# Splitting the squared activations inside the first MLP product instead of before the second

## What is computed

```python
h = x * (1 + sc2) + sh2
m = jnp.square(jax.nn.relu(h @ pl['w_mlp1'])) @ pl['w_mlp2']   # 1024 -> 4096 -> 1024
x = _layer_norm(DEEPNORM_ALPHA * x + g2 * m, pl['ln2_g'], pl['ln2_b'])
```

## Time and profile before

| quantity | value |
|---|---|
| median of 3 runs | 3762.24 us |
| the profiled execution | 3765.8 us, span 3764.0 us |
| PE busy | 3338.9 us (89% of the span) |
| VectorE busy | 2226.2 us (59%) |
| GpSimd busy | 1830.1 us (49%) |
| ScalarE busy | 1399.9 us (37%) |
| mean granted TensorE clock | 0.947 |
| DMA | 469.11 MB, mean 125 GB/s |

### The profile page before, as it was taken

How to read it: one execution, slowest core, us unless ns; L and a number is a source line. 1 busy time by engine, 2 the same in 40 slices (tenths; PEclk the granted TensorE clock), 3 DMA queues, 4 the chain that set the end, 5 groups by cost and what they waited for, 6 DMA issues and landing times. The chain is left out here.

```text
span 3764.0 us, 46756 instructions
## 1 busy us (share of the span) xinstructions
PE 3338.9 (89%) x17666; PEld 2793.2 (74%) x17666; DVE 2226.2 (59%) x2805; ACT 1399.9 (37%) x2366; POOL 1830.1 (49%) x1170
## 2 busy tenths in 40 slices
PE   7899997889599997898988999798887999888997
PEld 4677776777488886787867677677776888777876
DVE  3147555775923337888652774487575233588876
ACT  3212254772533224222252123477444233422224
POOL 3337554101566656655464574430126666566542
PEclk9999998999899998999999999899998999999998
DMA  8577637512122224222116764754212222522211
GB/s 276 213 232 234 202 117 197 119 68 86 62 91 92 96 99 156 84 89 71 60 50 238 226 208 156 198 118 121 92 42 71 96 100 91 180 68 84 94 52 56
DMA packets 312869, 469.11 MB, mean 125 GB/s; under 512 B 19895, under 2 KB 190117, under 8 KB 311366
## 3 DMA queue, kind: packets, MB, share of 16 engines
q1 hardware_dynamic: 239170, 313.30, 26.8%
q10 hardware_dynamic: 73476, 152.83, 12.0%
HBM read 325.81 MB, written 131.86 MB: 122 GB/s over the span
## 5 line engine op out<-in xcount | busy, mean ns | idle before, releaser
L3207 DVE SCALAR_TENSOR_TENSOR XT<-PS,ADA,XT 128x512 f32<-128x512 f32 (+1 forms) x552 | 346.0, 676 | 77.7 <-PE PS L1874 34.1
L1044 POOL TENSOR_TENSOR RH<-RAW,ONE 128x512 fp32r<-128x512 f32 x144 | 156.9, 1111 | 444.8 <-PE PS L1313 196.6
L1263 POOL TENSOR_TENSOR DAA<-DW,DAA 128x1024 fp32r<-128x1024 f32 x78 | 203.3, 2616 | 323.5 <-ACT DAA L2510 323.5
L1845 PE MATMUL PS<-HH,DAA 128*128 128x512 f32 x896 | 267.2, 417 | 77.6 <-DVE XT L3207 77.6
L1313 PE MATMUL PS<-HH,RH 128*128 128x512 f32 (+1 forms) x1208 | 279.5, 376 | 22.2 <-issue 13.6
L3156 DVE TENSOR_TENSOR UCC<-UCC,PS 128x512 f32<-128x512 f32 x96 | 66.0, 687 | 372.6 <-PE PS L1790 372.5
L1313 PEld LDWEIGHTS PS<-HH,RH 128*128 128x128 f32 x1208 | 209.5, 199 | 94.5 <-issue 61.9
L1845 PEld LDWEIGHTS PS<-HH,DAA 128*128 128x128 f32 x896 | 180.4, 204 | 121.8 <-DVE XT L3207 83.5
L3175 DVE TENSOR_TENSOR HL<-DRB,HH 128x1024 fp32r<-128x1024 f32 x92 | 214.3, 2332 | 79.2 <-ACT HH L2527 78.5
L1313 PE MATMUL PS<-HL,RH 128*128 128x512 f32 (+1 forms) x1208 | 258.2, 357 | 0.0
L1198 POOL TENSOR_TENSOR UOS<-TSS,UOS 128x512 fp32r<-128x512 f32 x128 | 165.8, 1296 | 182.5 <-ACT UOS L2493 180.8
(11 more groups left out here) (338 smaller groups left out, 8331.2 us busy)
## 6 DMA issues: line engine op xcount, KB each, us to landing
ADW<-in_w_ada_dram ACTq DMA_DIRECT2D x80, 512.0 KB, 5.6
UW<-in_w_mlp_dram SPq DMA_DIRECT2D x32, 1024.0 KB, 5.3
hidden_scratch<-UCC SPq DMA_DIRECT2D x128, 256.0 KB, 2.0
DW<-in_w_mlp_dram SPq DMA_DIRECT2D x32, 1024.0 KB, 4.9
DRB<-hidden_scratch SPq DMA_DIRECT2D x64, 512.0 KB, 3.6
RAW<-const_dram SPq DMA_DIRECT2D x52, 512.0 KB, 4.0
RAW<-in_w_in_dram SPq DMA_DIRECT2D x44, 512.0 KB, 4.9
z_scratch<-ZST ACTq DMA_DIRECT2D x40, 256.0 KB, 3.0
```

Of the source, the lines that this page charges most:

```text
L1044: nc.gpsimd.tensor_tensor(RH[:, s, part], RAW[:, p, part], ONE[:].broadcast_to([128, 512]), ALU.mult)\
L1263: P.tensor_tensor(d_a(name, 1), d_raw_a(name), d_a(name, 0).bitcast(F32), ALU.subtract)\
L1845: mm = pe.matmul(PS[:, d_bank(g, ph, j), :], d_a_tile(a, x, i, j), d_b_tile(g, b, y, i), start=(ph in ("P1", "P2", "P7") and n == 0 and i ...
L3207: V.scalar_tensor_tensor(x, PS[:, d_bank(g, ph, j), half:half + tn], ADA[:, A_G2 + k, COND[q]:COND[q] + 1], x, ALU.mult, ALU.add).then_inc ...
```

## The change

The squares stay in PSUM, and their block differences, high parts and low parts are made inside the first product. A pair now holds what one latent 2x2 block step of the second product needs: for pairs 0 to 13 the eight tiles B11, B22, B21, T1, T3, T2, T4, BP, and for pairs 14 and 15 the five tiles B11, B22, B21, B12, BP. ScalarE writes each tile's high part (`out_high`), VectorE its low part (`out_low`), into one of four buffers, "units", of 512 KB: two tiles UNIT0 and UNIT1, and two in the prompt columns of XT (named XU), whose content waits in DRAM meanwhile. A unit is stored to DRAM as one DMA and is free again when that has landed. Pairs 0 and 15 use only the first two units. The second product loads high and low parts straight into HH and HL. To match, the rows of w_mlp2 are dealt differently to the tiles, S1 has a buffer of its own, and the prompt tile's k order is swapped.

```diff
@@ sync engine
+                def store_out(p, name):
+                    unit = UNIT_OF[p, name]
+                    to = hid_d[p, IN_DRAM.index(name)]
+                    sp.wait_ge(h_made.sem, h_made.at(l, out_at(p, name)))
+                    if unit < 2:
+                        sp.dma_start(to, UNIT[unit][:].bitcast(F32)).then_inc(unit_out[unit].sem, 16)
...
+                def load_b(g, name):
...
+                    for part in range(2):
+                        sp.dma_start(d_b(g, name, part).bitcast(F32),
+                                     hid_d[2 * g:2 * g + 2, IN_DRAM.index(name), :, part, :].rearrange("t p n -> p t n"))\
...
                 for g in range(1, QUADS):
-                    for name, freed in (("BP", "BP"), ("B12", "T3"), ("B11", "T1"), ("B21", "T4")):
-                        sp.wait_ge(db_op.sem, db_op.at(l, d_made_b(g - 1, freed)))
-                        load_hidden(g, name)
+                    last = g == QUADS - 1
+                    if not last:
+                        load_b(g, "BP")
+                    load_b(g, "B11")
+                    load_b(g, "B21")
+                    if not last:
+                        load_b(g, "T2")
                     sp.wait_ge(da_sum.sem, da_sum.at(l, 4 * g))
                     load_rows(g, 1)
-                    sp.wait_ge(db_op.sem, db_op.at(l, d_made_b(g - 1, "B22")))
-                    load_hidden(g, "B22")
                     sp.wait_ge(da_op.sem, da_op.at(l, d_made_a(g - 1, "S1")))
                     load_rows(g, 0)
@@ tensor engine, first product
-                            pe.wait_ge(u_read.sem, u_read.at(l, u_read_at(p - 2, {"P1": "C12", "P7": "C21", "P2": "C11"}[ph])))
+                            pe.wait_ge(h_made.sem, h_made.at(l, out_at(p - 2, {"P1": "T3", "P7": "T4", "P2": "T1"}[ph])))
@@ tensor engine, before the second product
-                pe.wait_ge(u_read.sem, u_read.at(l, 6 * PAIRS))
+                pe.wait_ge(h_made.sem, h_made.at(l, len(OUTS)))
@@ scalar engine
-                def d_high_b(g, name):
...
+                def unit_free(p, name):
+                    unit = UNIT_OF[p, name]
+                    if stored_before(unit, p, name):
+                        act.wait_ge(unit_out[unit].sem, unit_out[unit].at(l, 16 * stored_before(unit, p, name)))
...
+                def result_out(p, name):
+                    relu(p, name)
+                    keep_result(p, name)
+                    out_high(p, name)
+
                 for p in range(PAIRS):
                     more = p + 1 < PAIRS
                     if p:
                         keep(p, "P1", 0)
+                        u_high(p, "A22")
+                        u_high(p, "A21")
+                        relu(p - 1, "BP")
                     keep(p, "P7", 1)
...
                     if more:
                         u_high(p + 1, "S2")
+                    result_out(p, "B11")
+                    if more:
                         u_high(p + 1, "S1")
...
+                    for name in U_OUT[p][3:-1]:
+                        out_high(p, name)
-                    if p == 1:
+                    if p == 0:
                         gains(l, 0, 2)
@@ vector engine
-                    V.scalar_tensor_tensor(x, x, 0.0, x, ALU.max, ALU.mult).then_inc(h_made.sem, 1)
...
+                def u_differences(p):
+                    h12, t1, t2, t4 = [PS[:, u_bank_of(p, name), :] for name in ("B12", "T1", "T2", "T4")]
+                    h11, h22, h21 = [UK[ph][:] for ph in ("P1", "P7", "P6")]
+                    V.tensor_tensor(t1, h12, h11, ALU.subtract).then_inc(u_raw_ready.sem, 1)
+                    C.link(V.tensor_tensor(h12, h22, h12, ALU.subtract))
+                    V.tensor_tensor(t2, h12, h11, ALU.add).then_inc(u_raw_ready.sem, 1)
+                    dve.wait_ge(u_raw_ready.sem, u_raw_ready.at(l, raw_at(p, "T3")))
+                    V.tensor_tensor(t4, h21, t2, ALU.subtract).then_inc(u_raw_ready.sem, 1)
...
                 for p in range(PAIRS):
                     u_combined(p, "C11")
+                    u_squared(p, "B11")
+                    out_low(p, "B11")
                     u_combined(p, "C22")
-                    u_squared(p, "R0")
+                    u_squared(p, "B22")
+                    out_low(p, "B22")
                     u_combined(p, "C21")
...
                 for g in range(QUADS - 1):
-                    for ph in D_PHASES:
-                        for j in range(8 if ph == "R" else 4):
-                            evacuate(g, ph, j)
-                        if g + 1 < QUADS - 1:
-                            d_low_b(g + 1, {"R": "BP", "P1": "B11", "P2": "B21", "P6": "T2", "P7": "T3", "P5": "T1",
-                                            "P4": "T4", "P3": "B22"}[ph])
...
+                    for ph, j in D_TILES:
+                        evacuate(g, ph, j)
```

More of the change, by code:

```diff
@@ L119, in u_read_at, with out_at, raw_at, stored_before @@
 def u_read_at(p, name):
-    return 6 * p + U_READS.index(name) + 1
+    return 3 * p + U_READS.index(name) + 1
+def out_at(p, name):
+    return OUTS.index((p, name)) + 1
+def raw_at(p, name):
+    return RAWS.index((p, name if name != "T2" else "T4")) + 1
+def stored_before(unit, p, name):
+    return sum(1 for x in OUTS[:out_at(p, name) - 1] if UNIT_OF[x] == unit)
+def in_unit(unit, pairs):
+    return sum(1 for x in OUTS if UNIT_OF[x] == unit and x[0] < pairs)
 def d_at(g, ph, j=None):
@@ L544, in d_prompt_tile, with u_unit, u_bank_of, shaped @@
         pair, q = b_slot(g, "BP")
-        at = 512 * q + 256 * (k % 2)
-        return (HH, HL)[part][:, 2 * pair + k // 2, at:at + 256]
+        at = 512 * q + 256 * (k // 2)
+        return (HH, HL)[part][:, 2 * pair + k % 2, at:at + 256]
+    def u_unit(p, name, part):
+        unit = UNIT_OF[p, name]
+        if unit < 2:
+            return UNIT[unit][:, part]
+        k = 4 * (unit - 2) + 2 * part
+        return XU[:, k:k + 2, LS:T]
+    U_KEPT_OF = {"B11": "P1", "B22": "P7", "B21": "P6"}
+    def u_bank_of(p, name):
+        own, other = U_BANK[p % 2], U_BANK[(p + 1) % 2]
+        return {"B11": own["c"], "T1": own["c"], "B22": other["d"], "T2": other["d"], "B21": own["b"], "T4": own["b"],
+                "B12": own["a"], "T3": own["a"], "BP": own["d"]}[name]
+    def shaped(z, unit):
+        return z.rearrange("p (a n) -> p a n", a=2) if unit > 1 else z
+    def u_result(p, name):
+        return shaped(PS[:, u_bank_of(p, name), :], UNIT_OF[p, name])
+    def u_scratch(p, name):
+        return "T1" if name == "B12" and p < PAIRS - 2 else name
+    def u_relu_views(p, name):
+        z = PS[:, u_bank_of(p, name), :]
+        if name in U_KEPT_OF:
+            return UK[U_KEPT_OF[name]][:], z
+        name = u_scratch(p, name)
+        return u_unit(p, name, 1).bitcast(F32), shaped(z, UNIT_OF[p, name])
     Q0, Q1 = slice(0, 512), slice(512, LS)
@@ L2644, in _ @@
                     else:
-                        for name in ("A12", "A21", "A22"):
-                            d_high(0, name)
-                        d_high_b(0, "BP")
-                    relu(p, "P3")
+                        d_high(0, "A11")
+                        d_high(0, "A12")
+                    result_out(p, "B21")
+                    relu(p, "B12")
                     if more:
                         u_high(p + 1, "S4")
-                    relu(p, "R1")
-                    if more:
-                        u_high(p + 1, "A22")
-                        u_high(p + 1, "A21")
-                    if p == 1:
-                        gains(l, 0, 2)
+                    for name in U_OUT[p][3:-1]:
+                        out_high(p, name)
+                    if p == 0:
+                        gains(l, 0, 2)
+                    if not more:
+                        d_high(0, "A21")
+                        d_high(0, "A22")
+                        relu(p, "BP")
+                        out_high(p, "BP")
                 def reloaded(n, j0, q):
@@ L2679, in _ @@
                     d_high(g, "S1")
[L2680 to L2690 removed]
+                    for name in D_MADE_A[g + 1][:-1] if g + 1 < QUADS - 1 else D_MADE_A[g + 1]:
+                        d_high(g + 1, name)
                 def norm_square(q, j):
@@ new lines, in u_combined @@
+                    part, ph, kept = {"C11": ("c", "P2", "P1"), "C22": ("a", "P5", "P7"), "C21": ("b", "P4", "P6")}[name]
+                    to = PS[:, other["d"] if name == "C22" else own[part], :]
+                    dve.wait_ge(u_phase.sem, u_phase.at(l, u_phase_at(p, ph)))
+                    dve.wait_ge(u_kept.sem, u_kept.at(l, 3 * p + ("P1", "P7", "P6").index(kept) + 1))
+                    V.tensor_tensor(to, UK[kept][:], PS[:, own[part], :], ALU.add).then_inc(u_read.sem, 1)
+                def u_squared(p, name):
+                    dve.wait_ge(u_relu.sem, u_relu.at(l, 5 * p + ("B11", "B22", "B21", "B12", "BP").index(name) + 1))
+                    r, z = u_relu_views(p, name)
```

(5 more changed lines are left out.)

300 lines of the change are left out of this document (126 added, 174 removed).

## The result

The changed kernel takes **3801.17 us** (median of 4 runs, 3790.55 to 3803.97) against 3761.77 us for the kernel before: ratio 1.0098, 95% interval 1.0078 to 1.0119. It is slower, as forecast, but by 39 us and not by 79. The profiled execution took 3799.58 us, its span is 3797.7 us against 3764.0 before, 33.7 us or 16.9 us per layer.

What follows compares the result with a forecast made beforehand. It took PE to bound the first product and VectorE's late evacuations to hold PE in the second. Terms of -15.8, +18.4, +18.7 and +17.9 gave +39.2 us per layer, +78.4 for two: 3841 us, range 3765 to 3892.

Steps and rivals of the forecast that it cites:

- The three signs: In the profile after: PE waiting mid-R for GpSimd's DAA, pairs stalling before P4, some 16 us standing before the first quad.
- the weights don't arrive in time: Rival, second product: loading plus GpSimd under 27.5 us, PE never waits in R, quads 49.6 us, kernel 3727 us; chance 0.13.
- the pair's chain: Rival, first product: handovers shorter by 1.5 us in sum, so the chain hides; kernel 3804 us; chance 0.10.
- the two ends: Rival, first pairs and transition: stores pass queued loads, units free early, 6 us each, kernel 3792 us; chance 0.12.
- the stores of a middle pair come back in time: Opposite of a rival: units come free too late, 28.0 us a pair, kernel 3885 us; chance 0.12.
- term 1: Second product's quads: late weights hold quads 1 to 6 at 59.1 us, quad 0 runs at 49.6; -15.8 us per layer.
- the step "GpSimd": Second product, chain from ScalarE's start behind the loading to A22's low part: 23.7 to 25.3 us, taken as 24.3.
- The loading: Second product: T2 and both row blocks of weights, 3.15 MB, land in 10.0 us.
- term 2: First product, pairs 2 to 14: a pair takes 26.3 us, not 24.84; +18.4 us per layer.
- the sum of handovers: First product, middle pair: engine steps counted from the copy of P1's sum, 14.6 us to P4, 26.3 to the next copy.
- Terms 3 and 4: Pairs 0 and 1, +18.7 us per layer; passage from first to second product, +17.9 us per layer.

Runs made afterwards that it cites:

- Experiments 6 and 7: 6: kernel before, VectorE's low parts of B operands cut short, 3689.69 us. 7: changed kernel, one extra VectorE SBUF subtraction per phase in quads 1 to 6, 3810.60 us.

## Why the prediction was right and wrong

**Right: the sign, what is late next, and where.** The three signs that it named are in the trace: a stall in the middle of R for DAA with the clock at 0.50 behind it, a stall before P4 that the read of C22 ends, and 17.5 us before the first quad with ScalarE waiting for a store. The rivals are out: the weights don't arrive in time (29.1 us of waiting), the pair's chain doesn't hide, the two ends cost 17.1 and 19.2 us and not 6, B11's store in the last pair didn't pass the loads ahead of it (11.3 us to land), and the stores of a middle pair come back in time (25.70 us and not 28.0). That 3801 lies beside the 3804 of the rival "the pair's chain hides" is chance: the pairs do have their stall, and the size comes from elsewhere.

**Wrong, term 1, the step "GpSimd".** "23.7 to 25.3; I take 24.3" was measured at 21.5 us: A11's high part starts at 1618.11 and A22's low part ends at 1639.6. Its terms were right in kind and wrong in size: 5.76 for A11 and A12 is 4.75, the sum S3 of 3.37 is 2.40, the lows S2 and S3 take 4.8. The larger values are rows of the kernel before, taken where VectorE worked in SBUF beside it, and that is the very work that the change removes. I saw this for two lows and not for A12 and the sum, so even my lower bound, 23.7, was too high. The loading, 10.0, measured 10.7. The loop is then 10.7 + 21.5 + 22.1 = 54.3 in place of 56.4, and the stall 4.7 in place of 6.8. With the slow clock a quad lasts 56.6 us in the mean (quad 1 starts at 1515.55, so 339.9 us for six; this one 57.15) and not 59.1: 6 x 2.45 = 14.7 us, the whole miss of the term. Experiments 6 and 7 show the cause from both sides. The prediction called 59.1 us "no better than now"; quads 1 to 6 had 56.7 in the mean before, so its own term meant them to become slower and all of the gain to come from quad 0.

The rule weighed in the prediction (the Trainium skill, page SBUF — State Buffer, section "SBUF: two separate sides": VectorE with two SBUF inputs and GpSimd lock each other out) was borne out, 3.39 against 2.40 us. I had applied it to the two lows alone; it covers A12's low and the sum S3 as well, and with these the chain comes down to what was measured.

**Wrong, term 2, the sum of handovers.** ScalarE's copy of P1's sum, PE's P4, and the next pair's copy in the changed kernel:

```profile
1321.28 0.60 ACT L2644 ACTIVATE UKP<-PS 128x512 f32<-128x512 f32 x1
1335.63 2.99 PE L1860 MATMUL PS<-XR,UOA 128*128 128x512 f32 x12 [0.63 <-DVE PS L3224]
1346.99 0.60 ACT L2644 ACTIVATE UKP<-PS 128x512 f32<-128x512 f32 x1
```

From the copy to P4 it counted 14.6 us, measured 14.35; from there to the next copy 11.7, measured 11.36. The second leg isn't a sum of handovers at all: the copy starts 2.95 us after its pair (1344.04), as before the change (2.94, from 1320.93 to 1323.87), where it waited for PE. So 11.36 is PE's own time for P4, P3, R1 and P1, and ScalarE's chain, which the prediction had closing the loop, is no longer than that. The two legs miss 0.25 and 0.34 us, 0.6 of 26.3, but PE's own pace of 24.84 is taken off first: of +1.46 a pair remained +0.86, which over 13 pairs is 7.8 of the 8.3 us missed. The mechanism of the stall was right: experiment 3 moves the one line that the working had named ("high S2 and then B11's relu"), and the pair is at 24.84.

**Terms 3 and 4** were off by 1.6 and 1.3 us. In pair 0 the stall was 5.92 (forecast +6.4 and the clock), pair 1's P6 waited for the copy behind the gains. At the transition 42.5 us were measured and 41.1 predicted; B12's relu started 36.0 us into the last pair (34 predicted), but ScalarE stood still twice, 5.63 us for B21's unit and 9.01 for B12's, and not once for 12.

The size of the whole was missed because it is a small difference of large terms: -16 of gain and +55 of loss per layer. Errors of 4% in a loop of 56 us and of 2% in a chain of 26 halved the result.

## What to carry to other kernels

A change that empties the bounding engine is worth what the next chain in *issue order* leaves of it: here four waits, each made by where one line stands (a load queued behind one that waits, a store behind loads, an operation behind one that needs another engine), turned a gain into a loss. Look for them in the queues before giving the change up: with the lines moved it is 2.8% faster than the kernel before. And durations taken from a profile in which two engines disturb each other don't hold once the change takes one of them away: look for the same operation where it ran alone.
